# Storing the FFN convolution states value by value from their channel layout, instead of turning them into rows in the last group

## What is computed

```python
h2 = rms_norm(x, norm_g[2])
gate, val = jnp.split(h2 @ w_up, 2, axis=-1)          # 2 x 3072 columns
gate_c, ffn_conv_new = causal_dwconv(gate, ffn_conv_h, ffn_conv_w, ffn_conv_b)   # 3 taps
f = (jax.nn.gelu(gate_c) * val) @ w_down
x = x + rms_norm(f, norm_g[3])
```

## Time and profile before

| | |
|---|---|
| median of 3 runs | 1471.04 us (1470.35 to 1471.28) |
| the profiled execution: its time | 1470.8 us |
| its span, first to last instruction | 1469.1 us |
| granted TensorE clock, mean over the span | 0.996 of full speed |
| PE busy, share of the span | 97% |
| DVE, ACT, POOL | 48%, 32%, 5% |

### The profile page before, as it was taken

The page is one execution under the profiler, slowest core; times in us unless marked ns, Lnnn a source line. Parts: engine busy times, 40 slices in busy tenths (PEclk is TensorE's granted clock), DMA queues, the critical chain, the costliest instruction groups (busy, mean ns, idle before and its releaser), DMA issues.

```text
span 1469.1 us, 20736 instructions
## 1 busy us (share of the span) xinstructions
PE 1431.3 (97%) x8521; PEld 1301.4 (89%) x8521; DVE 712.4 (48%) x1198; ACT 465.8 (32%) x686; POOL 74.7 (5%) x127
## 2 busy tenths in 40 slices
PE   7999999989999999999999999999999999999996
PEld 6999978956677889999999999999999999999895
DVE  6415443267786545535353535344444435353527
ACT  6324434066576434212121212121212121212023
POOL 3000002122000020000000000000000000000001
PEclk9999999999999999999999999999999999999998
DMA  7122113135414224211111111111111111111107
GB/s 244 63 58 58 51 61 112 62 95 183 143 45 144 86 87 129 58 29 58 29 57 29 57 29 56 29 55 31 45 40 36 50 29 57 29 57 29 43 1 177
DMA packets 80813, 100.32 MB, mean 68 GB/s; under 512 B 4474, under 2 KB 64667, under 8 KB 80614
## 3 DMA queue, kind: packets, MB, share of 16 engines
q1 hardware_dynamic: 71608, 67.73, 15.3%
q0 software_dynamic: 9152, 31.84, 6.9%
HBM read 82.93 MB, written 16.62 MB: 68 GB/s over the span
## 4 chain that ended last, share of the span: by engine, by line
PE 95%; DVE 3%; ACT 1%; DMA 0%; issue 0%; SPq 0%; ACTq 0%; DVEq 0%
PE PS L1554 51%; PE PS L1891 19%; PE PS L1859 6%; PE PS L1620 5%; PE PS L1544 4%; PE PS L1696 2%; PE PS L1771 2%; PE PS L1578 2%; PE PS L1813 1%; PE PS L1626 1%; DVE f_acc L1493 1%; PE PS L1719 1%; PE PS L1786 1%; DVE f_acc L1521 1%; DMA x_in<-in_x_prompt 0%
## 5 line engine op out<-in xcount | busy, mean ns | idle before, releaser
L1554 PE MATMUL PS<-act_hi,w_hi 128*128 128x384 f32 x1152 | 208.7, 335 | 0.0
L1554 PE MATMUL PS<-act_hi,w_lo 128*128 128x384 f32 x1152 | 207.9, 334 | 0.0
L1554 PE MATMUL PS<-act_lo,w_hi 128*128 128x384 f32 x1152 | 207.9, 334 | 0.0
L1554 PEld LDWEIGHTS PS<-act_hi,w_hi 128*128 128x128 f32 x1152 | 200.6, 188 | 0.9
L1554 PEld LDWEIGHTS PS<-act_lo,w_hi 128*128 128x128 f32 x1152 | 200.4, 188 | 0.0
L1554 PEld LDWEIGHTS PS<-act_hi,w_lo 128*128 128x128 f32 x1152 | 200.4, 188 | 0.0
L1493 DVE TENSOR_TENSOR f_acc<-f_acc,PS 128x512 f32<-128x512 f32 x216 | 145.2, 685 | 76.8 <-PE PS L1891 76.8
L1891 PE MATMUL PS<-w_hi,f_lo 128*128 128x512 f32 x432 | 168.3, 390 | 0.0
L1891 PE MATMUL PS<-w_lo,f_hi 128*128 128x512 f32 x432 | 168.3, 390 | 0.0
L1891 PE MATMUL PS<-w_hi,f_hi 128*128 128x512 f32 x432 | 168.2, 389 | 0.0
L1022 ACT ACTIVATE w_hi<-raw 128x1024 fp32r<-128x1024 f32 x72 | 72.1, 1049 | 225.5 <-PE PS L1891 219.5
(11 more groups left out here) (342 smaller groups left out, 1891.2 us busy)
## 6 DMA issues: line engine op xcount, KB each, us to landing
raw<-in_w_up SPq DMA_DIRECT2D x48, 512.0 KB, 4.6
raw<-in_w_down SPq DMA_DIRECT2D x24, 512.0 KB, 3.9
raw<-in_w_in SPq DMA_DIRECT2D x18, 512.0 KB, 4.6
x_in<-in_x_prompt SPq DMA_DIRECT2D x8, 512.0 KB, 3.8
raw<-in_w_out SPq DMA_DIRECT2D x8, 512.0 KB, 3.5
x_res<-in_x_prompt SPq DMA_DIRECT2D x8, 512.0 KB, 4.1
out_y_prompt<-x POOLq DMA_DIRECT2D x8, 512.0 KB, 5.0
out_y_prompt<-f_acc POOLq DMA_DIRECT2D x6, 512.0 KB, 8.9
```

The source lines that it names most:

```text
L1554: last = pe.matmul(PS[0:width, banks + c, 0:CW], w(wp, k), acts[ap][:, k, c * CW:(c + 1) * CW], start=(n == 0 and k == 0), stop=(n == 2 an ...
```

## The change

The turns on PE, the row copies on ACT and the four row stores on POOL go. POOL gets a loop over the 12 groups ahead of its accumulating stores. In group g it waits for `fconv_ready` of both tiles (DVE has written their states by then), and for each tile j issues two DMAs from `ffn_state[:, j, :]` straight to the outputs: 2 values on each of 128 partitions to `ffn_conv_p`, and 16 values on each to `ffn_conv_s`. In the outputs the 128 channels of a tile lie side by side, and the values of one partition lie 3072 values apart, so that each value is a piece of 4 bytes of its own. Nothing of `ffn_state` is overwritten, and no engine waits for these stores but POOL, at its very end.

```diff
+            state_out = [o[name].rearrange("l b k (j p) -> p j (l b k)", p=P) for name in ("ffn_conv_p", "ffn_conv_s")]
+
+            def store_states(g):
+                pool.wait_ge(fconv_ready, g * FG + FG)
+                for c in range(FG):
+                    j = g * FG + c
+                    for dst, r0, r1 in ((state_out[0], 0, FH), (state_out[1], FH, 18)):
+                        pool.dma_start(dst[:, bass.ds(j, 1), :], ffn_state[:, bass.ds(j, 1), r0:r1],
+                                       allow_slow_non_contiguous=True).then_inc(stored, 16)
+
+            with pool.Fori(0, NG) as g:
+                store_states(g)
             pool.wait_ge(x1_stored, 16 * NT)
             for t in range(NACC):
                 pool.wait_ge(f_normed, t + 1)
                 pool.dma_start(rows_of(yp, ys, t), f_acc[:, t, :], accum_op=ALU.add).then_inc(y_stored, 16)
-                if t == 0:
-                    pool.wait_ge(ffn_rows_ready, 6)
-                    for c0, part in ((0, state_rows_low), (2048, state_rows_high)):
...
             pool.wait_ge(y_stored, 16 * NACC)
-            pool.wait_ge(stored, 16 * 10)
+            pool.wait_ge(stored, 16 * (6 + 2 * FT))
...
-            def state_rows_out(c):
-                act.wait_ge(ffn_turned, c + 1)
-                part, c0 = (state_rows_low, c * 512) if c < 4 else (state_rows_high, (c - 4) * 512)
-                act.activation(part[:, c0:c0 + 512], PS[0:18, 6 + c % 2, :], ACT.Copy).then_inc(ffn_rows_ready, 1)
...
-            def turn_states(c):
-
-                if c == 0:
-                    pe.wait_ge(added, (NG - 1) * 18 + 18)
-                if c >= 2:
-                    pe.wait_ge(ffn_rows_ready, c - 1)
-                for k in range(4):
-                    last = turn(PS[0:18, 6 + c % 2, k * P:(k + 1) * P], ffn_state[:, 4 * c + k, :])
-                last.then_inc(ffn_turned, 1)
...
-                if is_last:
-                    pe.wait_ge(fconv_ready, FT)
-                    turn_states(5)
-                    pe.wait_ge(ffn_rows_ready, 5)
...
-                    if is_last and q == 1:
-                        pe.wait_ge(ffn_rows_ready, 6)
```

More of the change, by code:

```diff
@@ L340, in encoder_step @@
         state_rows = probs_t[:, 1, 512:1024]
-        state_rows_low = raw[0:18, :, :].rearrange("p a b -> p (a b)")
-        state_rows_high = gains[0:18, 1, :]
         PS = ctx.enter_context(nc.psum_tensor("PS", [P, 8, 512], F32))
@@ L484, in encoder_step @@
         y_last = sem("y_last")
-        ffn_turned = sem("ffn_turned")
-        ffn_rows_ready = sem("ffn_rows_ready")
         stored = sem("stored")
@@ L1089, in ffn_group @@
                     ffn_tile(g * FG + c, c)
[L1090 to L1093, removed]
                     if not more and c == FG - 1:
-                        state_rows_out(4)
                         act.activation(stat[:, TMP:TMP + 1], stat[:, EPSC:EPSC + 1], ACT.Sqrt)
-                        state_rows_out(5)
                     ffn_hi(g * FG + c, c)
-                    if not more and c == 0:
-                        state_rows_out(2)
-                        state_rows_out(3)
                     if more:
```

## The result

The changed kernel takes **1492.7 us** (median of 4 runs, 1491.1 to 1496.1) against 1470.85 us beside it (4 runs, 1470.35 to 1471.28): ratio 1.0151 [1.014, 1.0163], 22 us slower. The prediction of 1468.1 us (1467.3 to 1471.0) was wrong in sign. The profiled execution took 1496.1 us, its span is 1494.4 us. That is 25.3 us more than the 1469.1 us of before.

What follows compares the result with a forecast made beforehand. The prediction took PE to bound the kernel (busy 97% of the span), with DVE pacing the tail. Removing PE's 2.91 us and adding 0 for hidden stores gave 1471.04 - 2.91 = 1468.1 us, range 1467.3 to 1471.0.

Steps and rivals of the forecast that it cites:

- Removed on PE: PE, last group: without the transposes it becomes a plain group, 77.38 - 74.47 = 2.91 us gained.
- Rival 2: PE, last group: only the bare transposes go, 2.30 us, giving 1468.7 us; chance 0.12.
- Nothing on PE or DVE becomes late: Last group and tail: DVE keeps 1.3 us of cover, and the whole tail moves up by 2.91 us.
- POOL's issues: POOL in the FFN: four stores take 4.0 us of a 74.47 us group, while POOL stands idle 879.90 us.
- The price of the transfers: DMA engines, each group: 288 values per engine, 2.2 to 15.8 us, some 6 us taken; no cost while hidden.
- high end: Transfers: the forget gates' whole 3.5 us landing charged to one engine's 64 pieces, 55 ns each, 15.8 us per group.
- low end: Transfers: from the software queue's 9.0% share during the forget gates' stores, 7.5 ns per piece, 2.2 us per group.
- Cover (a): Groups 0 to 10: engines 16% busy, weights 13 us ready, so PE would notice only far above 55 ns per value.
- Covers (b) and (c): Last group: 18.3 us before the first accumulating store, and 4.3 us between the last one's landing and the span's end.
- Rival 1: POOL's and DMA queues at the tail's start: stores slower than 78 ns per value, 1480 us at 120 ns; chance 0.08 slower.
- Rival 3: Tail: held by full DMA engines, not DVE; values overlapping the accumulating stores would give 1469 to 1471 us; chance 0.05.
- Rival 4: Last group: time only moves elsewhere, by slower clock or instruction fetch, 1471.0 us; chance 0.02.

Runs made afterwards that it cites:

- e1: The changed kernel without any store of the FFN convolution states (these two outputs left out): 1467.48 us, ratio 0.9978 against the kernel before.
- e3: The changed kernel with only the last group's states stored value by value, those of groups 0 to 10 left out: 1493.53 us, ratio 1.0153.
- e6: The changed kernel storing only the last group, to scratch with neighbouring partitions' values 64 bytes apart, rows 8 KB apart: 1467.4 us, ratio 0.9979.
- e5: The changed kernel storing only the last group, to scratch with neighbouring partitions' values 4 bytes apart, rows 512 bytes apart: 1478.72 us, ratio 1.0055.
- e4: The changed kernel storing only the last group, to scratch where every 4-byte value has 256 bytes of its own: 1466.58 us, ratio 0.9977.
- e11: The changed kernel with all twelve groups stored to scratch, neighbouring partitions' values 64 bytes apart, states missing from the outputs: 1467.53 us, ratio 0.9983.
- e9: The changed kernel storing only the last group, to scratch with one partition's values 8 bytes apart, partitions not side by side: 1474.3 us, ratio 1.0027.
- e8: The changed kernel with `ffn_state` relaid, four PE transposes after the last convolution, two ACT copies, two DMAs of 512-byte rows: 1467.83 us, ratio 0.9981.

## Why the prediction was wrong, step by step

- **Removed on PE: right.** Last matmul to last matmul is 1457.11 - 1382.64 = 74.47 us, as forecast, and e1 is 3.1 us faster (2.91 forecast). Rival 2 (2.30 us only) is out.
- **Nothing on PE or DVE becomes late: right.** DVE's chain from the first add moved up with PE in e1.
- **POOL's issues: right.** A store of 256 values takes 0.71 us and one of 2048 values 1.17 (forecast 0.59 and 1.41), a group 3.76 us (4.0).
- **The price of the transfers: this step failed.** Its bounds were 7.5 to 55 ns per value and engine, from pieces of 16 bytes, and it took 20. In the loop, from the first store at 1051.02 to ACT's next weights at 1092.81, it is 41.8 us for 288 values per engine: 145 ns, or 132 with the load's usual 3.9 us taken off. In the last group, from 1426.71 to `x_back` at 1476.8 it is 50.1 us, or (50.1 - 5.6) / 288 = 155 ns with the load's own time taken off; this is rather too much, since from 1460 us on the accumulating stores move beside the load. So the high end was too low by 2.4 to 2.8 times. It was called "the worst reading of the nearest row" although no row had pieces of 4 bytes, and the range excluded what nothing had measured.
- **The low end came from a reading that is blind.** It took the share of the stores' own queue for what they cost (9.0%). The same reading gives 7 ns for the stores of e3 and for those of e6. The landing, from which the high end came, does tell them apart (20.4 us in e5, 5.0 in e6), and the prediction leaned away from it.
- **The nearest row had neighbours too.** The kernel writes the forget gates of rows 6 with those of neighbouring partitions 16 bytes apart, so that four pieces share 64 bytes. They landed in 3.5 us, where 132 ns for each of an engine's 64 pieces would be 8.4. So to share 64 bytes isn't enough to be slow. It takes the smaller piece (4 bytes), or more of them side by side, or something else in which these stores differ; no run here separates that.
- **"Hidden three times": incomplete.** Cover (a) held almost wholly: the weights came up to 32 us late for ACT, and PE lost nothing in all groups but two. Covers (b) and (c) looked at POOL's accumulating stores alone. These did land 21 us later (30.0 against 8.9 us), but what DVE waited for was SP's `x_back`, issued 6.3 us after the first state store and asked for 24.7 us later (1457.78). The list of who else moves data in that stretch lacked it, and lacked the final stores (5.2 us).
- **The rivals.** Rival 1 had the direction, with chance 0.08. Its threshold of 78 ns was passed by 1.7 to 2 times. At 132 to 155 ns its sum gives 1484 to 1490, which comes near the result, partly by luck: the place was another. Rival 3 named values in flight among the accumulating stores, which came true, but priced them at 1469 to 1471. Rival 4 is out: with the stores left out (e1) nothing is lost.
- **The row stores, counted as nothing.** In e1 the span ends 2.4 us behind DVE's last operation, before 3.0, so their going may be worth some 0.5 us.
- **The rules of the Trainium skill.** The estimate from its pages "DMA: Bandwidth & Descriptors" and "VectorE: DVE Perf Modes" (0.9 us per group by a 19 times slower copy) is off by more than 40 times here. The Trainium skill's page "DMA: Bandwidth & Descriptors", Rules for kernel authors, calls for a rearranged last dimension, and as advice it was right: the row version is faster. The read, modify and write of pieces below 512 bytes in the Specifications of the same page of the Trainium skill doesn't tell the cases apart: e4, e6 and e11 write pieces of 4 bytes too, without a loss.
- **What tells them apart** is the distance of the values: 4 or 8 bytes apart they hold the load up (e3, e5, e9), 64 or 256 bytes apart hardly (e4, e6, e11). Two readings of that stay open. In e3, e5 and e9 values share 64 bytes, and in e4, e6 and e11 none do; but in e4, e6 and e11 every value also starts at a multiple of 64 bytes from the tensor's start, and in the others most values don't.

**Still open.** What stops PE in the middle of an up product for 1.6 us (1.58, and 1.26 + 0.30) in two groups of the changed kernel: the profile names no releaser, DVE stands at the same moment, and neither e11 nor before has it, so it comes with the slow stores, but by which path no run shows. Twice POOL's second pair of stores in a group comes 28 to 29 us behind the first with no releaser named (at 858.59 and at 1383.00), 28 stores apart. In e11 POOL stands before the same two pairs, but for 3.6 to 3.7 us:

```profile
833.49 1.87 POOL L805 DMA_DIRECT2D state_scratch<-ffn_state  x2 [3.70 <-issue]
```

So where it stands doesn't depend on the addresses, and how long goes with the speed of the stores. It looks like a queue that holds so many stores and no more, which wasn't tested. Also open are the 15 us between rows 512 bytes and 12 KB apart, and where between 8 and 64 bytes the slowdown ends, since no distance between them was run.

## What to carry to other kernels

Before scattering small values to HBM, ask which of them land side by side: 4608 values of 4 bytes kept the next load back until 42 to 50 us after their first store when they lay side by side, and delayed it by 1.9 us (7.7 against 5.8) when they lay 64 bytes apart. Such stores hold the other queues too, so price them against every queue's transfers in that stretch and against the deadline of each, not only against what stands behind them on their own queue. Where no row has the access pattern of the new transfer, its high end is unknown, and the share of its own queue is no price at all: leave it open in the range, or turn the data on PE first, where four transposes (three of 128 columns, one of 48) cost 0.35 us.

## What the hardware showed that was not expected

- **A busy queue can be an innocent one.** The share of q1 doubled (15.3% to 32.3%) with the same packets and bytes, while q0, which carried the stores, went from 6.9% to 8.3%. Nor do packets count values: q0 has 10944 - 9024 = 1920 packets more than in e1, which leaves these stores out (9024 on its page), for 55,296 values.
- **The accumulating stores land sooner with nothing between them.** Without the four row stores of before they land in 5.8 us (e1) and not in 8.9. In e8, whose two row stores are issued 8 us ahead of them, it is 6.8.
- **A further small piece costs POOL little to issue**: 1.17 - 0.71 = 0.46 us for 1792 more, 0.26 ns each.
